# One decoder layer on one core: four square roots of a recurrence put off, its scans cut in two pieces and spread over later attention groups

## What is computed

```python
# group A: gated linear recurrence over time
r  = sigmoid(xb @ w_ra + b_ra);  gi = sigmoid(xb @ w_ix + b_ix)
log_a = -8 * softplus(-lam) * r;  a = exp(log_a)
inp = sqrt(-expm1(2 * log_a)) * gi * x          # h[t] = a[t] * h[t-1] + inp[t]
out_a = gelu(gr) * h
# group B: an indexer scores all keys, the 256 best are attended to (8 query heads, 2 key heads)
score = sum_h iw_h * relu(iq_h . ik);  idx = top_k(score, 256)
out_b = softmax(q . k[idx] / 8) @ v[idx]
# both: group norm, one output projection, residual, SwiGLU feed-forward of width 2816
mix = concat(rms(out_a), rms(out_b)) @ w_out
```

## Time and profile before

| what | value |
|---|---|
| time of three runs, median (lowest to highest) | 1303.21 us (1301.89 to 1303.48) |
| the profiled execution, its own time | 1303.42 us |
| its span, first to last instruction | 1301.4 us |
| mean granted TensorE clock | 0.987 |
| PE, DVE, ACT, POOL busy, share of span | 97%, 66%, 52%, 57% |

### The profile page before, as it was taken

How to read it: one execution, slowest core, us unless ns; L and a number is a source line. 1 busy time by engine, 2 the same in 40 slices (tenths; PEclk the granted TensorE clock), 3 DMA queues, 4 the chain that set the end, 5 groups by cost and what they waited for, 6 DMA issues and landing times.

```text
span 1301.4 us, 25300 instructions
## 1 busy us (share of the span) xinstructions
PE 1261.2 (97%) x9537; PEld 1157.9 (89%) x9537; DVE 854.9 (66%) x1595; ACT 671.0 (52%) x1152; POOL 739.5 (57%) x477
## 2 busy tenths in 40 slices
PE   6899999988899999999999999999999999999998
PEld 4777999876766767999999999999999999999998
DVE  6777889889677748577973554555545562644595
ACT  5657888968776766455442333433334336211115
POOL 2242448990242103456587787887878857765620
PEclk8899999999899999999999999999999999999999
DMA  9823116432101126655322253433534269998633
GB/s 340 291 68 75 50 47 212 148 130 81 50 17 34 46 73 226 192 164 152 103 89 65 99 181 133 176 105 124 196 130 165 88 238 319 332 344 332 241 127 131
DMA packets 128298, 198.86 MB, mean 153 GB/s; under 512 B 16839, under 2 KB 100111, under 8 KB 117680
## 3 DMA queue, kind: packets, MB, share of 16 engines
q1 hardware_dynamic: 128032, 193.01, 43.2%
q10 hardware_dynamic: 144, 4.23, 0.8%
HBM read 144.07 MB, written 53.18 MB: 152 GB/s over the span
## 4 chain that ended last, share of the span: by engine, by line
PE 71%; DVE 8%; ACT 5%; POOLq 5%; POOL 3%; DVEq 3%; issue 2%; SPq 1%; ACTq 1%; DMA 1%
PE ps L3548 30%; PE ps L3568 15%; PE ps L3232 2%; PE ps L3246 2%; PE ps L3412 2%; ACT junk L1387 2%; PE ps L3414 2%; PE ps L3413 2%; PE ps L3221 1%; DMA ada_part<-in_ada_w 1%; POOLq L1101 1%; PE ps L3222 1%; DVE junk L2123 1%; DVEq L2673 1%; PE ps L3365 1%
## 5 line engine op out<-in xcount | busy, mean ns | idle before, releaser
L3568 PE MATMUL ps<-input,down_H 128*128 128x258 f32 x1120 | 180.6, 283 | 1.8 <-DVE acc L2821 1.8
L3568 PEld LDWEIGHTS ps<-input,down_H 128*128 128x128 f32 x1120 | 154.5, 190 | 2.4 <-issue 1.4
L3548 PE MATMUL ps<-comb,opH 128*128 128x258 f32 x960 | 154.4, 283 | 0.0
L1195 POOL TENSOR_TENSOR opL<-wsum,opH 128x512 fp32r<-128x512 f32 x80 | 124.0, 1559 | 36.0 <-ACT opH L1723 32.7
L1723 ACT CAST opH<-wsum 128x512 fp32r<-128x512 f32 x80 | 49.6, 621 | 168.0 <-PE ps L3548 114.6
L3548 PEld LDWEIGHTS ps<-comb,opH 128*128 128x128 f32 x960 | 132.7, 190 | 0.0
L3548 PE MATMUL ps<-h2H,opH 128*128 128x258 f32 x640 | 129.0, 283 | 0.3 <-DVE h2L L2678 0.3
L3548 PE MATMUL ps<-h2H,opL 128*128 128x258 f32 x640 | 129.0, 283 | 0.0
L3548 PE MATMUL ps<-h2L,opH 128*128 128x258 f32 x640 | 128.6, 282 | 0.0
L1038 POOL TENSOR_TENSOR wL<-wraw,wH 128x1024 fp32r<-128x1024 f32 x28 | 69.8, 2494 | 87.2 <-ACT wH L1380 86.7
L2821 DVE TENSOR_TENSOR acc<-ps,acc 128x516 f32<-128x516 f32 x112 | 76.6, 694 | 62.0 <-PE ps L3568 61.4
(11 more groups left out here) (528 smaller groups left out, 3535.3 us busy)
## 6 DMA issues: line engine op xcount, KB each, us to landing
down_inputs<-staged SPq DMA_DIRECT2D x35, 1032.0 KB, 4.8
input<-down_inputs SPq DMA_DIRECT2D x35, 1032.0 KB, 6.2
adb<-in_ada_w SPq DMA_DIRECT2D x8, 2048.0 KB, 8.4
wraw<-in_w_out SPq DMA_DIRECT2D x24, 512.0 KB, 4.5
raw<-in_w_gate SPq DMA_DIRECT2D x10, 1024.0 KB, 6.6
raw<-in_w_up SPq DMA_DIRECT2D x10, 1024.0 KB, 5.1
down_block<-in_w_down SPq DMA_DIRECT2D x5, 2048.0 KB, 10.8
ada_part<-in_ada_w SPq DMA_DIRECT2D x3, 2048.0 KB, 15.7
```

Source lines behind the costliest of these rows:

```text
L1195: pool.tensor_tensor(opL[g % OPS][:], operand(v, p), opH[g % OPS][:].bitcast(F32), ALU.subtract).then_inc(s_wL, 1)
L3548: ins = mm(ps[:, sum_bank(v, p) + h, 0:HC], weight[s][:, k, :], token[:, k, h * HC:(h + 1) * HC], start=begins, stop=ends, skip_group_chec ...
L3568: ins = mm(ps[:, 2 * m + h, 0:HC], weight[:, f, cc], tok[:, f, part, h * HC:(h + 1) * HC], start=(f == 0 and weight is hi and part == 0), ...
```

## The change

Five things, all between the front and the end of the attention. The four square roots move behind `unit(7)`'s start: roots 0 and 1 no longer stand between `unit_evac(6)` and `gate_r(2)`, and DVE's `rooted` calls move with them. The tanh of tile 0 goes ahead of the wait for the last convolution; tiles 2 and 3 go through tanh, exp and square one by one. The ties of the selection with 768 keys leave the front for groups 0 to 4, and those with 896 keys and 1024 keys take other groups. Scan 0 leaves the front too, and every scan is two pieces, placed at groups 8 to 13; the last piece of scan 3 stands in group 13, where it was in group 11. Buffers are laid out again to allow this, and SP loads the pages 7, 6, 3 in this order, with the wait for the last `rooted` ahead of 6. The instructions on PE and POOL keep their order.

```diff
-SCAN_AT = {8: 1, 9: 2, 11: 3}
+SCAN_AT = {8: ((0, 0),), 9: ((0, 1),), 10: ((1, 0),), 11: ((1, 1), (2, 0)), 12: ((2, 1),), 13: ((3, 0), (3, 1))}
...
-EARLY_TIES = 4
+EARLY_TIES = 3
 EARLY_W = P * (FIRST_SEL + EARLY_TIES)
-TIE_AT = ((2, 4, 5, 6), (6, 7, 10, 10), (12, 12, 13, 13))
+TIE_AT = ((0, 2, 3, 4), (5, 6, 7, 7), (8, 9, 10, 10), (12, 12, 13, 13))
...
-        pinv = sb("pinv", [P, NLG])
+        pinv = keyL[:].rearrange("p a n -> p (a n)")[:, 0:NLG].bitcast(F32)
...
-        gi = (spare[0][:], root3[:], spare[0][:], gel[:, 3, :])
-        gt = (spare[1][:], gel[:, 3, :], spare[1][:], root3[:])
+        root2 = at("root2", [P, NTOK], RING + 16512)
         root3 = at("root3", [P, NTOK], RP + 33920)
+        gi = (spare[0][:], root3[:], root3[:], spare[0][:])
+        gt = (spare[1][:], gel[:, 3, :], root2[:], spare[0][:])
+        squared_decay = (spare[0][:], root3[:], root3[:], root3[:])
...
# SP
-            for b in (6, 7):
+            pages(kpg, "cache_k", s_pg, 7)
+            sp.wait_ge(s_gx, 9)
+            for b in (6, 3):
                 pages(kpg, "cache_k", s_pg, b)
-            sp.wait_ge(s_gx, 9)
-            pages(kpg, "cache_k", s_pg, 3)
...
# ACT
             act.wait_ge(s_wL, 8)
             gate_r(1)
             gate_i(1)
+            act.drain()
+            decay_tanh(0)
             act.wait_ge(s_xc, 4)
-            decays(0)
+            decay_tanh(1)
+            act.drain()
+            decayed(0)
+            decayed(1)
+            act.drain()
             decay_squared(0, 2)
             decay_squared(1, 3)
             A(dsm[:, 7:8], consts[0:64, C_ONE:C_ONE + 1], ACT.Gelu_apprx_tanh)
             unit_evac(6)
-            root(0)
-            root(1)
             A(dsm[:, 7:8], consts[0:64, C_ONE:C_ONE + 1], ACT.Sigmoid)
             gate_r(2)
+            act.wait_ge(s_lu, 2)
             gate_i(2)
             gate_r(3)
+            gate_i(3)
+            act.drain()
+            decay_tanh(2)
+            act.drain()
+            decayed(2)
+            act.drain()
+            decay_squared(2, 4)
             act.wait_ge(s_gx, 5)
-            gate_i(3)
-            decays(2)
-            decay_squared(2, 6)
-            decay_squared(3, 7)
+            decay_tanh(3)
+            act.drain()
+            decayed(3)
+            act.drain()
+            act.wait_ge(s_lu, 3)
+            decay_squared(3, 5)
...
             first_keys_high(0)
-            root(2)
+            root(0)
             first_keys_high(1)
             q_high(0)
+            root(1)
+            first_keys_high(2)
+            root(2)
             root(3)
-            first_keys_high(2)
             q_evac(0)
             A(dsm[:, 7:8], consts[0:64, C_ONE:C_ONE + 1], ACT.Gelu_apprx_tanh)
+            act.wait_ge(s_gx, 7)
             unit_evac(7)
...
# DVE
-            def scan(c):
+            def scan(c, part):
 
                 a, h = ga[c], conv_out(c)
-                V.tensor_tensor(a[:, T:NTOK], a[:, T:NTOK], stT[:, c:32:4], ALU.mult)
-                V.tensor_tensor_scan(h[:, 0:T], a[:, 0:T], h[:, 0:T], 0.0, ALU.mult, ALU.add)
-                dve.drain()
+                if part == 0:
+                    dve.wait_ge(s_gx, 1 + LT + c + 1)
+                    V.tensor_tensor(a[:, T:NTOK], a[:, T:NTOK], stT[:, c:32:4], ALU.mult)
+                    V.tensor_tensor_scan(h[:, 0:T], a[:, 0:T], h[:, 0:T], 0.0, ALU.mult, ALU.add)
+                    dve.drain()
+                    return
                 V.tensor_tensor(h[:, T:NTOK], h[:, T:NTOK], a[:, T:NTOK], ALU.add)
                 V.tensor_copy(lasts[:, c:c + 1], h[:, T - 1:T])
                 dve.drain()
...
+                if g == NLG - 1:
+                    dve.wait_ge(s_gx, 1 + 2 * LT)
...
             ties(2)
-            rooted(0)
-            rooted(1)
             ada_row_late(ADA_1 + 6)
-            dve.wait_ge(s_lev, 6)
-            scan(0)
             gated(2)
             gated(3)
-            ties(3)
             root_input(2)
             root_input(3)
             ada_row_late(ADA_1 + 7)
             first_keys_low(0)
-            rooted(2)
+            rooted(0)
             first_keys_low(1)
             q_low(0)
+            rooted(1)
+            first_keys_low(2)
+            rooted(2)
             rooted(3)
-            first_keys_low(2)
...
-                if n in SCAN_AT:
-                    scan(SCAN_AT[n])
+                for c, part in SCAN_AT.get(n, ()):
+                    scan(c, part)
```

More of the change, by code:

```diff
@@ L284, in build @@
         RH, RP = base, base + 2 * KD * NTOK * 4
-        size = 2 * KD * NTOK * 4 + 146688 + 1024 + 160
+        size = 2 * KD * NTOK * 4 + 146688 + 1024 + 224
         ctx.enter_context(nc.sbuf_tensor("arena", [P, size // 4], F32))
@@ L296, in build @@
         RING = RP + 60352
-        Q5 = RING + 37024
+        Q5 = RING + 37088
         x0T = at("x0T", [P, KD, NTOK], RING)
@@ L329, in build @@
         lraw = [at(f"lraw{i}", [P, KD, P], RING + 4128 * i) for i in range(SLOTS)]
-        lH = [at(f"lH{i}", [P, KD, P], RING + 12384 + 8192 * i, F32R) for i in range(SLOTS)]
-        lL = [at(f"lL{i}", [P, KD, P], RING + 12384 + 8192 * i + 4096, F32R) for i in range(SLOTS)]
+        lH = [at(f"lH{i}", [P, KD, P], RING + 12448 + 8192 * i, F32R) for i in range(SLOTS)]
+        lL = [at(f"lL{i}", [P, KD, P], RING + 12448 + 8192 * i + 4096, F32R) for i in range(SLOTS)]
         ikT = at("ikT", [P, 2, T], RING, F32R)
@@ L371, in build @@
         ga = [at(f"decay{c}", [P, NTOK], RING + 4128 * c) for c in range(LT)]
-        spare = [at(f"spare{i}", [P, NTOK], RING + 28768 + 4128 * i) for i in range(2)]
+        spare = [at(f"spare{i}", [P, NTOK], RING + 28832 + 4128 * i) for i in range(2)]
+        root2 = at("root2", [P, NTOK], RING + 16512)
         root3 = at("root3", [P, NTOK], RP + 33920)
-        gi = (spare[0][:], root3[:], spare[0][:], gel[:, 3, :])
-        gt = (spare[1][:], gel[:, 3, :], spare[1][:], root3[:])
+        gi = (spare[0][:], root3[:], root3[:], spare[0][:])
+        gt = (spare[1][:], gel[:, 3, :], root2[:], spare[0][:])
+        squared_decay = (spare[0][:], root3[:], root3[:], root3[:])
         csum = at("conv_sum", [P, NTOK], RP + 29760)
@@ L1435, in decay_squared @@
                 act.wait_ge(s_gx, gated)
-                A(gi[c], ga[c][:], ACT.Square).then_inc(s_a2, 1)
+                A(squared_decay[c], ga[c][:], ACT.Square).then_inc(s_a2, 1)
             def root(c):
@@ L1440, in root, with decay_tanh @@
                 A(gt[c], gt[c], ACT.Sqrt).then_inc(s_lq, 1)
[L1442 to L1449, removed]
+            def decay_tanh(c):
+                A(gt[c], ga[c][:], ACT.Tanh, scale=nsp[:, 1, c:c + 1])
             for u in range(NU_LRU - 3):
@@ L2216, in root_input @@
                 dve.wait_ge(s_a2, c + 1)
-                stt(gt[c], gi[c], 1.0, gt[c], ALU.add, ALU.mult).then_inc(s_lu, 1)
+                stt(gt[c], squared_decay[c], 1.0, gt[c], ALU.add, ALU.mult).then_inc(s_lu, 1)
             def rooted(c):
```

## The result

The changed kernel takes 1317.37 us (median of 4 runs, 1315.39 to 1318.78) where the kernel before took 1303.35 beside it: a ratio of 1.0104, 95% interval 1.0089 to 1.0118. That is 1.0% slower, inside the forecast of 1314 to 1326 and 2.6 us under its middle. The profiled execution took 1317.77 us with a span of 1315.7, against 1303.42 and 1301.4 before: +14.3.

The account below looks back on a forecast made before the run. It took SP's page queue, bound by SP's issuing behind the last scan, as decisive. With the earlier gain already in the 17.3 us delay, 1303.4 + 14.8 + 2.0 = 1320.2, called 1320; range 1314 to 1326.

Parts of the forecast that it names:

- The front, -4.1: Stages before the attention: moved roots and earlier tanh save 4.1 us, between -4.6 and -3.0.
- PE's own shift: Front, on PE: `unit(7)` starts 4.6 us sooner, as the products of tile 3 no longer wait.
- My sum of ACT's list: End of the front: ACT's added durations put the gelu of unit 7 at 329.4 instead of 333.54.
- `gate_i(2)` costs nothing: Front, on ACT: its new wait for `root_input(1)` ends at 305.7, before its own product at 306.05; 0.35 us of cover.
- The attention, -1.1: Group 8: an earlier mask shortens PE's idling and perhaps spares the clock, -1.1 us, between -0.7 and -2.1.
- The scan's end, 450.8: Group 13, DVE: last scan ends at 450.8 instead of 433.5, queue 17.3 us later; trace sign 450 to 452.
- The queue, 56.5 us: SP: 56.5 us from last scan to first weight load, landing 4.7 later; ACT's cast +14.8 after 2.5 of slack.
- The clock, +2.0: Page work on PE after some 19 us of idling: lower granted clock costs 2.0 us, between 0 and 7.8.
- the case above 1326: Whole kernel: a time above 1326, some 1329; chance 5%.
- the queue hides: Rival, SP's queue: weights come in time and the 5.2 us gain stays, giving 1298; chance 7%.
- DVE's fuller groups: Rival, attention: late masks eat the front's gain while the queue is hidden, giving 1303; chance 3%.
- The part that I priced at nothing: Attention: 768-key ties add 4.4 us to DVE while 896-key steps leave two groups; net nothing, between -1 and +1.

Follow-up runs that it names:

- e2: The kernel before with only its last scan moved from group 11 to group 13: 1325.20 us, ratio 1.0156.
- e1: The changed kernel with only the scan table put back to earlier groups, the last three pieces in group 11: 1298.19 us, ratio 0.9947.
- e9: The changed kernel, scans as late, with SP loading six sets of page numbers ahead, five before its wait for the first scan: 1295.70 us, ratio 0.9935.
- e10: Control: the kernel before with the same loads of page numbers ahead: 1304.38 us, ratio 1.0004.
- e2b: The kernel before with only its last scan moved from group 11 to group 12: 1315.31 us, ratio 1.0079.
- e6: e5 with the ties of 768 keys back in the front: 1298.72 us, ratio 0.9954.
- e5: The changed kernel with its scan pieces spread over groups 1 to 11, one piece a group: 1299.87 us, ratio 0.9964.
- e11: e9 with the ties of 768 keys back in the front: 1294.05 us, ratio 0.9916.

## Why the prediction was right, point by point

**Bound and mechanism** stood as forecast: the queue is late by the scan, ACT stands in order before the cast, PE before the page copy. Shown by e2 (the scan alone makes the wait), e1 and e9 (without a late queue the time is gained), e10 (the queue was no bound before).

**The front, -4.1**, measured -4.96, right in mechanism and 0.9 too small. PE's own shift is -5.27 (314.36 to 309.29, less the 0.20 by which the changed execution runs late), not -4.6: the 0.4 us by which the first matmul of `unit(7)` gets ahead of the last products stood in my old time and not in my new one. PE's longer wait at the front's end, 1.41 us instead of 1.05, gives 0.36 back. My sum of ACT's list gave the gelu at 329.4; it stands at 328.77. That `gate_i(2)` costs nothing held (306.35, behind PE's product).

**The attention, -1.1**, measured -2.28, just outside its own ends (-0.7 and -2.1). In group 8 the idling is 1.20 us, not 2.10, and the clock didn't fall (1.00 from 395 on, against 0.83 before). Counted as in the table, the lead is -5.61 at the last pair of masks ahead of that wait (394.08 before), -6.52 at the next pair (404.25) and -7.24 at group 13: 0.65 come ahead of it, 0.91 with it and 0.72 behind it, where the clock's part and that of the fuller groups aren't told apart.

**The scan's end, 450.8**, measured 448.8. This follows from the two terms above: 7.0 us sooner, not 5.2. That is before the 450 to 452 that I named as the sign. The queue starts 15.3 us later, not 17.3.

**The queue, 56.5 us**, measured 506.63 - 448.8 = 57.8, and the landing 4.5 instead of 4.7. ACT's cast came at 511.11, +13.9 against 497.22 where I had +14.8. Two mis-sized terms (2.0 too late, 1.3 too short) went against each other, so that the sum is nearer than its parts is luck.

**The clock, +2.0**, measured 1.6. Its size doesn't follow the length of the idling: e2b lost 3.0 us behind 6.0 of idling, e2 2.4 behind 18.9. No run shows my upper end of 7.8, where all the page work takes twice its time and which the case above 1326 needs as well: in the changed kernel the eight transposes and twelve products at its end took 1.10 and 3.83 us, as before (1.09 and 3.83), and the largest loss in any run was the 3.0 us of e2b. The first output product is 15.5 us later (508.27 to 523.77), and 1.2 of it is back by the end of the span; where, I haven't shown.

**The rivals.** That the queue hides was excluded by 20.84 us of ACT's idling; its price of 1298 was near what e1 gave once the condition was met. DVE's fuller groups cost nothing: PE gained there. The part that I priced at nothing between bounds of -1 and +1 was a net of two: the 768-key ties that come into groups 0 to 4 and the other ties that leave. The net is the -0.65 above, inside the bounds. The first half by itself costs more than they allow, between first mask and group 13 1.8 us on the spread scans (e6 against e5) and 1.6 on the late ones (e11 against e9). So by difference the rest, above all the other ties that leave, gave some 2.3 us (an estimate, 1.6 + 0.65); no run tried it alone.

## What to carry to other kernels

Before an instruction is moved later, ask which queue starts on its semaphore, and follow that queue to its last transfer: here DVE had room for the scan two groups later, and 57.8 us of SP's issuing hung on it. A queue of transfers can be bound by what its engine does between them (here, with the page numbers held, the same 64 took 34.6 us instead of 57.8), and then work whose inputs have long been there (address registers) belongs in that engine's idle time. And when a large gain upstream shows up as nothing or a loss, count the lead at several points from a common event: the lead was there up to 490 us, and one wait then took nearly three times as much.

## What the hardware showed beside this

Page numbers cost SP about 2.55 us for eight registers, as much as five of its transfers (0.51 us apart). In the changed kernel a table switch shows as its load alone, 1.28 us: the load at 299.36 starts 0.02 us behind the end of the activation ahead of it (298.29 + 1.05), and the next one starts at 300.65, as it ends. A granted clock of 0.66 appeared once (e6) in 5 us in which PE was never idle and DMA moved 261 GB/s; what caused it stays open.
